# A two-block transformer kernel: the split of the second block's input moved into the last feed-forward tiles, scale sums behind the first group, two small steps shifted by a group or a tile

## The reference, cut to what matters

```python
# RWKV-7 time mix: the keys are normalised per head
kk = heads(k * k_k)
kk = kk / jnp.maximum(jnp.linalg.norm(kk, axis=-1, keepdims=True), 1e-12)
...
# end of the first block, and its norm
h = h + conv_ffn(rms_norm(h, norm_ffn[l]), ffn_up[l], ffn_conv_w[l], ffn_conv_b[l], ffn_down[l])
return rms_norm(h, norm_final)
...
# start of the second block: norm of a norm, then one wide projection
h = rms_norm_2(x, g_attn[l])
z = h @ w_in[l]
...
# relative bias of the window and summary attention, from a table of 32 buckets
bias_win = tbl_heads[:, rel_bucket(win_dist)].reshape(G, R, Q_BLOCK, Q_BLOCK + WINDOW)
```

## Time and profile before

| | us |
|---|---|
| median of 3 runs | 2133.32 |
| lowest and highest run | 2125.81, 2134.75 |
| profiled execution, its own time | 2132.3 |
| profiled execution, span from first to last instruction | 2130.5 |

### The profile page before, as it was taken

How to read it: one execution, slowest core, us unless ns; L and a number is a source line. 1 busy time by engine, 2 the same in 40 slices (tenths; PEclk the granted TensorE clock), 3 DMA queues, 4 the chain that set the end, 5 groups by cost and what they waited for, 6 DMA issues and landing times. The chain is left out here.

```text
span 2130.5 us, 29579 instructions
## 1 busy us (share of the span) xinstructions
PE 2033.2 (95%) x11736; PEld 1616.3 (76%) x11736; DVE 1077.9 (51%) x1813; ACT 801.8 (38%) x1303; POOL 133.7 (6%) x173
## 2 busy tenths in 40 slices
PE   8999879989999998999999989999999999999997
PEld 6678647858887877888888767886666778888886
DVE  5566375464445535477775244228555554423433
ACT  5432352243323424344443222326555534412421
POOL 0000136600000000000000000000000000000000
PEclk9999989989999999999999989999999999999998
DMA  4133200013222430233333422222111132222332
GB/s 174 65 114 119 89 14 9 3 58 113 93 95 90 131 127 21 89 99 97 91 98 111 165 88 89 90 90 66 35 40 40 60 99 89 97 93 97 99 99 79
DMA packets 48594, 181.96 MB, mean 85 GB/s; under 512 B 5504, under 2 KB 5888, under 8 KB 47840
## 3 DMA queue, kind: packets, MB, share of 16 engines
q1 hardware_dynamic: 44240, 165.61, 23.9%
q0 software_dynamic: 3088, 12.90, 1.8%
q10 hardware_dynamic: 1152, 1.89, 0.3%
HBM read 175.08 MB, written 5.29 MB: 85 GB/s over the span
## 5 line engine op out<-in xcount | busy, mean ns | idle before, releaser
L209 DVE TENSOR_TENSOR weights_lo<-weights_raw,weights_hi 128x1024 fp32r<-128x1024 f32 (+2 forms) x288 | 363.5, 1262 | 813.2 <-ACT weights_hi L201 813.0
L201 ACT ACTIVATE weights_hi<-weights_raw 128x1024 fp32r<-128x1024 f32 (+2 forms) x288 | 313.4, 1088 | 857.2 <-PE sp_ps L234 257.0
L232 PE MATMUL sp_ps<-arena_parts,weights_hi 128*128 128x512 f32 x720 | 283.3, 394 | 3.0 <-DVE arena_parts L293 2.5
L234 PE MATMUL sp_ps<-arena_parts,weights_lo 128*128 128x512 f32 x720 | 280.9, 390 | 0.0
L233 PE MATMUL sp_ps<-arena_parts,weights_hi 128*128 128x512 f32 x720 | 280.9, 390 | 0.0
L232 PE MATMUL end_ps<-arena_parts,weights_hi 128*128 128x512 f32 x576 | 224.8, 390 | 2.2 <-DVE arena_parts L3124 1.7
L234 PE MATMUL end_ps<-arena_parts,weights_lo 128*128 128x512 f32 x576 | 224.1, 389 | 0.0
L233 PE MATMUL end_ps<-arena_parts,weights_hi 128*128 128x512 f32 x576 | 224.1, 389 | 0.0
L232 PE MATMUL fr_ps<-arena_parts,weights_hi 128*128 128x512 f32 (+1 forms) x480 | 182.7, 381 | 6.7 <-DVE arena_parts L293 2.4
L233 PE MATMUL fr_ps<-arena_parts,weights_hi 128*128 128x512 f32 (+1 forms) x480 | 181.1, 377 | 0.0
L234 PE MATMUL fr_ps<-arena_parts,weights_lo 128*128 128x512 f32 (+1 forms) x480 | 181.0, 377 | 0.0
(11 more groups left out here) (388 smaller groups left out, 3047.6 us busy)
## 6 DMA issues: line engine op xcount, KB each, us to landing
weights_raw<-w_up SPq DMA_DIRECT2D x44, 512.0 KB, 3.4
weights_raw<-w_proj SPq DMA_DIRECT2D x38, 512.0 KB, 3.5
weights_raw<-w_gates SPq DMA_DIRECT2D x32, 576.0 KB, 3.7
weights_raw<-w_ca SPq DMA_DIRECT2D x32, 512.0 KB, 3.4
weights_raw<-w_down SPq DMA_DIRECT2D x16, 704.0 KB, 4.2
weights_raw<-w_in SPq DMA_DIRECT2D x22, 512.0 KB, 3.4
weights_raw<-w_logits SPq DMA_DIRECT2D x16, 512.0 KB, 3.5
weights_raw<-w_ff1a SPq DMA_DIRECT2D x16, 512.0 KB, 3.5
```

The lines of the kernel that those rows point to most:

```text
L201: act.activation(self.w_hi[:, g % 2, 0:cols], self.raw[:, g % 2, 0:cols], ACT.Copy).then_inc(self.hi_ready, 1)
L209: dve.tensor_tensor(self.w_lo[:, g % 2, 0:cols], self.raw[:, g % 2, 0:cols], self.w_hi[:, g % 2, 0:cols].bitcast(F32), ALU.subtract).then_ ...
L232: pe.matmul(out, left[0], right[0], start=start, stop=False)
L234: return pe.matmul(out, left[1], right[0], start=False, stop=stop)
```

## The change

`norm_sums` stands behind group 9 instead of 8, and VectorE takes it at n == 9, ahead of `invert` in the same step. In the feed-forward stage half 0 of the relative bias stands behind tile 3 instead of 4, and ScalarE's part at step 5 instead of 7. `Residual` has a new argument `ahead`, the split of the second block's input: pairs 0 to 6 are made at the last two steps of the stage (behind the first half of the last tile), pair 7 behind the last addition. On VectorE the last two additions of squares move ahead of these pairs, and the lowering of the second projection group moves behind the last addition to `h`. A second new argument `final` gives the last sum and the last square tiles 31 and 30, since the pairs take tiles 68 to 70. PE runs group 0 of the projection ahead of the sums and spreads the scales behind group 2; the steps of ScalarE and VectorE shift by one group to match. The gains are made ahead of the feed-forward stage, and ScalarE waits for them there.

```diff
@@ -686,7 +686,7 @@
                         tm.loras(pe, n - 4)
-                    if n == 8:
+                    if n == 9:
                         tm.norm_sums(pe)
...
@@ -810,9 +810,8 @@
                         tm.sum_up(dve, (6, 8, 10, 11).index(n))
-                    if n == 8:
+                    if n == 9:
                         tm.take_norm(dve)
-                    if n == 9:
                         tm.invert(dve)
...
@@ -1418,8 +1417,9 @@
     def __init__(self, core, name, phase, rhs, ps, per_tile=1, squares=None, beside=None, source=None, gained=None, following=None,
-                 lowered=None):
+                 lowered=None, ahead=None, final=None):
         self.core, self.phase, self.rhs, self.ps = core, phase, rhs, ps
+        self.ahead, self.final = ahead, final
         self.per_tile, self.squares, self.beside, self.gained, self.following = per_tile, squares, beside, gained, following
...
@@ -1447,10 +1447,10 @@
         deep = lambda n, lowered=None: pe_gemm_deep(self.core, pe, n, self.per_tile, PHASES[self.phase][1], self.rhs, self.ps, lowered)
-        deep(4, self.lowered)
+        deep(3, self.lowered)
         if self.beside:
             self.beside.tensor(pe, 0)
-        deep(2)
+        deep(3)
         if self.beside:
...
@@ -1462,10 +1462,11 @@
                 self.following.hi(act, d)
-
+            if self.ahead and d == KD - 1:
+                self.ahead.hi(act, d)
             if d >= 3:
                 act.wait_ge(self.added, d - 2)
-            to = squares[min(d, 1 + (d + 1) % 2)]
+            to = self.final[1] if self.final and d == KD - 1 else squares[min(d, 1 + (d + 1) % 2)]
             act.activation(to, core.h[:, d, :], ACT.Square).then_inc(self.squared, 1)
...
@@ -1477,10 +1478,14 @@
             core.split_hi(act, self.g0 + n + 2)
-            if self.beside and n == KD * self.per_tile // 2 - 1:
+            if self.beside and n == 3 * self.per_tile - 1:
                 self.beside.scalar(act)
...
                 square(n // self.per_tile - 1)
+            if self.ahead and n == KD * self.per_tile - 2:
+                act.wait_ge(self.beside.taken, HEADS + 2)
+                for k in range(KD - 1):
+                    self.ahead.hi(act, k)
         if squares:
...
@@ -1491,7 +1496,8 @@
                 dve.wait_ge(self.added, d - 1)
-            dve.tensor_tensor(squares[0], squares[0], squares[1 + (d + 1) % 2], ALU.add).then_inc(self.added, 1)
+            to = self.final[0] if self.final and d == KD - 2 else squares[0]
+            dve.tensor_tensor(to, squares[0], squares[1 + (d + 1) % 2], ALU.add).then_inc(self.added, 1)
...
@@ -1502,7 +1508,16 @@
         for n in range(KD * self.per_tile):
-            core.split_lo(dve, self.g0 + n + 2)
+            last = self.ahead and n == KD * self.per_tile - 1
+            if last:
+                dve.wait_ge(core.groups_done, self.g0 + n)
+                add_squares(KD - 2)
+                add_gained(KD - 2)
+                dve.wait_ge(self.added, KD - 2)
+                for k in range(KD - 1):
+                    self.ahead.lo(dve, k)
+            else:
+                core.split_lo(dve, self.g0 + n + 2)
             if (n + 1) % self.per_tile == 0:
...
@@ -1510,6 +1525,9 @@
                    .then_inc(core.banks_free, 1)
+                if last:
+                    core.split_lo(dve, self.g0 + n + 2)
+                    break
                 if squares and d >= 2:
...
@@ -1518,6 +1536,8 @@
             self.following.lo(dve, KD - 1)
+        if self.ahead:
+            self.ahead.lo(dve, KD - 1)
...
@@ -2587,9 +2607,10 @@
         down = Residual(core, "down", "down", lambda k: core.pair(0, NF, k), ps, per_tile=2, squares=squares_of(68)(core), beside=bias,
-                        gained=([core.arena[:, 71 + n, :] for n in range(2)], "norm_final"), lowered=up.lower_done)
+                        gained=([core.arena[:, 71 + n, :] for n in range(2)], "norm_final"), lowered=up.lower_done,
+                        ahead=split, final=(a[:, 31, :], a[:, 30, :]))
         g0, e0 = core.plan(22, 16)
-        first = TokenScale(core, "sp_first", [a[:, 68 + n, :] for n in range(2)], ps_v[:, 0, :], first_scale, a[:, 9, :], 56)
+        first = TokenScale(core, "sp_first", [a[:, 31, :], a[:, 30, :]], ps_v[:, 0, :], first_scale, a[:, 9, :], 56)
         both = TokenScale(core, "sp_both", [a[:, 71 + n, :] for n in range(2)], ps_v[:, 1, :], token_scale, a[:, 10, :], 60)
...
@@ -2622,15 +2643,16 @@
                 x = lambda k: core.pair(XN_HI, XN_LO, k)
+                pe_gemm(core, pe, 1, KD, x, ps, lowered=split.lowered)
                 down.squares_final(pe)
...
                 both.sums(pe)
-                pe_gemm(core, pe, 2, KD, x, ps, lowered=split.lowered)
-                first.spread_out(pe)
-                both.spread_out(pe)
-                for n in range(2, 16):
+                for n in range(1, 16):
                     pe_gemm(core, pe, 1, KD, x, ps)
+                    if n == 2:
+                        first.spread_out(pe)
+                        both.spread_out(pe)
                     if n == 3:
...
@@ -2663,20 +2685,17 @@
                 up.scalar(act)
+                act.wait_ge(gains_ready, 1)
                 down.scalar(act)
...
                 small.load(act)
-                act.wait_ge(gains_ready, 1)
-                act.wait_ge(bias.taken, HEADS + 2)
-                for k in range(KD):
-                    act.wait_ge(core.banks_free, down.taken(k))
-                    split.hi(act, k)
-                first.root(act)
-                both.root(act)
-                small.raise_up(act)
                 for n in range(22):
...
                     if n == 0:
+                        first.root(act)
+                        both.root(act)
+                        small.raise_up(act)
+                    if n == 1:
                         first.keep(act)
...
@@ -2707,14 +2726,12 @@
                 up.vector(dve)
-                down.vector(dve)
                 first_gain, second_gain = [core.vec[:, VEC_AT[x]:VEC_AT[x] + KD] for x in ("norm_final", "g_attn_2")]
...
                 dve.wait_ge(gains_ready, 1)
-                split.lo(dve, 0)
+                down.vector(dve)
                 first.mean(dve)
-                for k in range(1, 3):
-                    split.lo(dve, k)
+                core.split_lo(dve, g0 + 2)
                 first.invert(dve)
...
@@ -2722,16 +2739,13 @@
                 dve.tensor_scalar(both.inverse, both.inverse, 1.0 / D, RMS_EPS, ALU.mult, ALU.add).then_inc(both.mean_ready, 1)
-                for k in range(3, 5):
-                    split.lo(dve, k)
                 dve.wait_ge(both.rooted, 1)
...
                 both.place(dve, both.inverse)
-                for k in range(5, KD):
-                    split.lo(dve, k)
+                small.lower(dve)
...
@@ -2742,12 +2756,12 @@
-                for n in range(22):
+                for n in range(1, 22):
                     core.split_lo(dve, g0 + n + 2)
-                    if n == 0:
-                        small.lower(dve)
+                    if n == 1:
                         dve.wait_ge(both.ready, 1)
                         dve.wait_ge(first.ready, 1)
+                        take(0)
                     if n < 16:
...
```

## The result

The changed kernel takes 2119.94 us (median of 8 runs, 2115.99 to 2121.42) against 2133.55 us of the kernel before (8 runs, 2125.81 to 2135.49). The ratio is 0.9943, with a 95% interval of 0.9930 to 0.9957: 13.6 us at the median, 12.2 by the ratio, between 9 and 15. Forecast were 15.7 us and 2117.6. The profiled execution took 2121.15 us with a span of 2119.4 (before 2132.3 and 2130.5).

What follows compares the result with a forecast made beforehand. TensorE (PE), busy 95% of the span, was taken as the bound. Gains of 10.8 (second gating) and 4.9 (key norm), 15.7 us, take the profiled 2132.3 to 2116.6; 1.0 for the median gives 2117.6, range 2110 to 2125.

Steps and rivals of the forecast that it cites:

- Part 1, does the early work fit: Second gating: seven early pairs ready in time, eighth with 1.0 us margin, so the first projection group follows without a gap.
- Part 1, the price of the sums: Second gating: 32 one-column passes cost 3.4 us of the 14.20 lost there, so 10.8 us gained.
- The rule against the change: Half-rate clock is the default, array activity releases it; 32 one-column passes are hardly activity, giving the first rival's sum.
- the first rival: Clock falls within the second gating's new sums: 5.5 us less gain, 10.2 in all, 2123.1 us; chance 0.12.
- Parts 2 to 5: Later scale spread, DMA queues, earlier gains wait, earlier bias rows: nothing gained or lost; bias rows at worst half a microsecond.
- Part 6: Key norm sums behind group 9: wait gone, eight passes at full clock in 3.45 us, 4.9 us gained, chain late for nothing.
- The sum: Second gating's 10.8 plus key norm's 4.9 make 15.7 us gained over the whole kernel.
- The chances: Whole kernel: faster 0.82, within 0.5% (10.7 us) 0.16, slower 0.02; the forecast itself 0.73.
- PE would wait for the last pair: Second gating: lower halves start 3 us later, PE stands 2 us in the first group; 3 to 4 lost, 2121; chance 0.06.
- the norm chain would give its gain back: Key norm: root or reciprocal holds VectorE over 6 us more, group 12 waits, 4.9 us lost, 2122.5; chance 0.05.
- a weight group would starve: Projection weight group 3 lands late behind the compression weights, PE stops behind the spread; 2135 us or more; chance 0.02.
- the split would not be early: A wait keeps the seven pairs behind the feed-forward's end; about 8 us gained in all, 2125; chance 0.02.

Runs made afterwards that it cites:

- the kernel with 24: Changed kernel with 8 idle one-column passes ahead of the first scale's 16 behind group 0, the second scale's 16 behind group 1: 2116.77 us, one run.

## Why the prediction was right or wrong

Faster was forecast with 0.82, and the time lies in the range (2110 to 2125), 2.3 us above the forecast. By its steps:

- **Part 1, does the early work fit.** Right. The margin was 1.4 us, not 1.0; the seven lower halves take 4.72 us from the first start to the last end, and the addition starts at 1265.48, 0.85 us behind the first group's start (forecast 1.2).
- **Part 1, the price of the sums.** This is the term that was mis-sized. The passes cost 3.49 us, as taken (3.4). What I left out at the value I took was the row's effect on what follows: 1.71 us of slow products. The place gained 14.20 - 3.49 - 1.71 = 9.0 us, not 10.8; the distances say the same (54.5 - 45.5). I had argued from 16 passes at full clock to 32, and the kernel with 24 shows that this step does not hold; the last norm shows that even 16 don't always leave the clock up.
- **The rule against the change, and the first rival.** The rule pointed the right way: the clock fell with PE never idle. The rival's picture, clock 0.50 within the sums and 5.5 us lost, was too dark: it fell behind them and cost 1.7. The truth lay between forecast and rival. The Trainium skill, "TensorE: Matmul & The Clock Gate", part 1, ties the full clock to activity of the array; the trace agrees, and shows that a queue of one-column passes without a gap did not keep it.
- **Parts 2 to 5.** Right: no wait of PE between the sums and the small logits; the projection group asked for beside POOL's transfers took 10.1 us to land in place of 10.5 and nobody waited for it; the feed-forward stage takes 135.92 us with the bias rows at either place.
- **Part 6.** Right at 4.9: 4.8 us in the trace, 4.9 in the kernel with this part alone. The chain behind it was shorter than I had it, since the table load ran ahead of the wait.
- **The sum.** 9.0 + 4.8 = 13.8, against 13.6 between the medians and 12.2 by the ratio. That the first two agree so closely is partly luck, for the two profiled executions differ by 11.1 only. I followed the same product through both traces. The changed kernel's lead grows by 4.7 us at the key norm, by 1.6 at the norm spreads behind it (two stretches of half clock before, one after) and by 9.0 at the second gating. It shrinks by 2.4 in the stick-breaking attention and by 1.6 behind the last norm's sums; the rest makes 0.2 less. No edit touches the attention (mean granted clock 0.80 in 70 us of the trace before, 0.78 in the same 70 of the trace after), and the three traces of the changed kernel differ there among themselves, so this part is chance between executions. The fall behind the last norm stands in all three traces of the changed kernel and not in the one before. If it comes with the change, 13.8 - 1.6 = 12.2 us are left, as by the ratio; with one trace of the kernel before, that is not shown. The windows of the attention, before and after:

```profile
...
250.00:320.00 70.00, 48.48 (x250) 28.05 (x248) 48.23 (x68) 37.31 (x87) 24.83 (x31) 0.80 0.09 30
...
```

```profile
...
246.00:316.00 70.00, 47.67 (x237) 26.71 (x237) 46.91 (x67) 37.20 (x86) 24.28 (x31) 0.78 0.09 28
...
```

- **The chances.** The outcomes that the prediction puts beyond 0.5% have chances of 0.73 and 0.06, which make 0.79 and not 0.82. Nothing above hangs on it.

The rivals that PE would wait for the last pair, that the norm chain would give its gain back, that a weight group would starve, and that the split would not be early are excluded by PE's timeline and the list of its waits.

## What to carry to other kernels

Where an engine that is busy for 95% waits for a short side computation, put a full group of its own work between the inputs of that computation and its use, and check that the other engines can then feed both; here either half of the move alone was worth a quarter of the whole. Price side work on TensorE not only by its own time but by what the products behind it run at. Breaking a row of thin passes up between groups can pay: 16 and 16 cost 1.5 us less than 32 here. It is no guarantee, since 16 at the last norm brought slow products in nine of 14 traces; look for each stretch of half clock in the whole trace after such a change. Two profiled executions can differ by a few microseconds of clock in stages that nobody touched, so compare the distance around the change, not only the spans.

## What the runs showed of the hardware that I had not expected

- The granted clock fell to 0.50 behind 24 (one trace) and 32 one-column passes (five traces) with PE busy without a gap before and after, and within a row of 48 (one trace). Behind 16 in the second gating it stayed at 1.00 (three traces, and the second 16 of the 24-pass kernel); behind the last norm's 16 it fell in nine of 14 traces.
- It also falls within or behind the eight norm spreads, whose operands have 8 rows each, in all 14 traces. In the kernel before, the spreads take 4.41 us and the 12 products from 97.94 take 5.25; in the changed one they take 3.62 and the 12 from 92.70 take 4.44, where full clock is 2.72. Two stretches of half clock in place of one also stand in three traces with the norm sums late, so the 1.6 us between these two traces can't be put down to the change.

```profile
...
93.53 4.48 PE L473 MATMUL proj_ps_v<-arena 8*128 8x512 f32 x8
97.94 0.80 PE L232 MATMUL proj_ps<-arena_parts,weights_hi 128*128 128x512 f32 x1
...
103.19 0.40 PE L232 MATMUL proj_ps<-arena_parts,weights_hi 128*128 128x512 f32 x1
...
```

```profile
...
89.08 3.70 PE L473 MATMUL proj_ps_v<-arena 8*128 8x512 f32 x8
92.70 0.50 PE L232 MATMUL proj_ps<-arena_parts,weights_hi 128*128 128x512 f32 x1
...
97.14 0.40 PE L232 MATMUL proj_ps<-arena_parts,weights_hi 128*128 128x512 f32 x1
...
```

- ScalarE's table load ran ahead of the wait of the root that needs it: at 76.30, 1.80 us before the maximum was even begun at 78.10, while the root itself started at 78.81.
